# A ring of six joined rows instead of eight in the PEER layer, with the gate and gelu products made at the end of their own group

## What is computed

```python
def peer_block(xb, w_query, sub_keys, u_tab, v_tab):
    ...
    s1, i1 = lax.top_k(s[:, :, 0], PEER_TOPK)
    s2, i2 = lax.top_k(s[:, :, 1], PEER_TOPK)
    cand_s = (s1[..., :, None] + s2[..., None, :]).reshape(T, PEER_HEADS, PEER_TOPK * PEER_TOPK)
    ...
    top_s, pos = lax.top_k(cand_s, PEER_TOPK)
    e = jnp.take_along_axis(cand_i, pos, axis=-1)
    gate = jax.nn.softmax(top_s, axis=-1)
    act = jax.nn.gelu(jnp.einsum('thkd,td->thk', u_tab[e], xb).astype(jnp.float32))
    return jnp.einsum('thk,thkd->td', (gate * act).astype(xb.dtype), v_tab[e])
```

## Time and profile before

| | |
|---|---|
| time, median of 3 runs | 4445.95 us (4445.74 to 4453.35) |
| the profiled execution | 4451.51 us, of which the span of the profile is 4449.7 us |
| PE matmul busy | 3031.3 us (68%) |
| DVE busy | 2706.4 us (61%) |
| POOL busy | 1379.5 us (31%) |
| ACT busy | 1113.9 us (25%) |
| mean granted TensorE clock | 0.813 of full speed |
| moved by DMA | 1226.80 MB, of which 1132.54 MB by GpSimd's queue |

### The profile page before, as it was taken

The page is one execution under the profiler, slowest core; times in us unless marked ns, Lnnn a source line. Parts: engine busy times, 40 slices in busy tenths (PEclk is TensorE's granted clock), DMA queues, the critical chain, the costliest instruction groups (busy, mean ns, idle before and its releaser), DMA issues.

```text
span 4449.7 us, 52623 instructions
## 1 busy us (share of the span) xinstructions
PE 3031.3 (68%) x18622; PEld 1384.5 (31%) x18622; DVE 2706.4 (61%) x6853; ACT 1113.9 (25%) x2691; POOL 1379.5 (31%) x1229
## 2 busy tenths in 40 slices
PE   6999895377746766676676676676576666667656
PEld 3554342166624322222222222232132222222211
DVE  1710666633343767767767767776776776676775
ACT  1010342222112222322222322222232232222222
POOL 0000000000001544544444454453454444444421
PEclk8999787589868787787887788788778788778778
DMA  2111000000016999999999999999999999999974
GB/s 84 36 34 44 3 0 9 0 20 0 1 47 259 400 406 406 391 413 404 390 416 408 389 413 405 389 413 410 383 408 408 407 389 410 398 390 413 397 284 152
DMA packets 203348, 1226.80 MB, mean 276 GB/s; under 512 B 31424, under 2 KB 42336, under 8 KB 67584
## 3 DMA queue, kind: packets, MB, share of 16 engines
q0 software_dynamic: 160256, 1132.54, 62.9%
q1 hardware_dynamic: 42880, 91.61, 5.7%
HBM read 1211.00 MB, written 13.06 MB: 275 GB/s over the span
## 4 chain that ended last, share of the span: by engine, by line
DMA 30%; PE 14%; DVE 13%; issue 7%; POOL 5%; ACT 1%; SPq 0%; POOLq 0%; DVEq 0%; ACTq 0%
DMA uv_rows<-in_peer_uv,expert 29%; PE peer_y L1747 10%; POOL uv_rows L1294 4%; DVE uv_rows L1491 4%; PE peer_s L1632 2%; ACT diag L1613 1%; DVE same L1340 1%; DVE same L1338 1%; DVE pick L1342 1%; DVE p_x L1382 1%; PE peer_y L1741 1%; PE beside L1646 1%; PE peer_y L1721 0%; POOL pages_ring L1273 0%; DVE where L1318 0%
## 5 line engine op out<-in xcount | busy, mean ns | idle before, releaser
L1747 PE MATMUL peer_y<-uv_rows,diag 64*64 64x512 f32 x8192 | 1366.2, 801 | 973.6 <-ACT diag L1613 973.1
L1491 DVE CUSTOM_DVE_ANT_0 uv_rows<-uv_rows,p_h 128x1024 f32<-128x1024 f32 x1056 | 1293.0, 1225 | 760.5 <-DMA uv_rows<-in_peer_uv,expert 743.6
L1294 POOL DMA_INDIRECT uv_rows<-in_peer_uv,expert x1056 | 1215.3, 1151 | 1625.8 <-PE peer_y L1747 1083.5
L1747 PEld LDWEIGHTS peer_y<-uv_rows,diag 64*64 64x64 f32 x8192 | 333.0, 167 | 1773.6 <-ACT diag L1613 1247.6
L1613 ACT ACTIVATE diag<-p_ident,weights 128x128 f32<-128x128 f32 x1024 | 355.0, 394 | 1448.1 <-DVE weights L1366 1442.5
L328 PE MATMUL proj<-mix,w_in_tile 128*128 128x512 f32 x672 | 296.2, 599 | 19.4 <-issue 19.4
L1632 PE MATMUL peer_s<-wk,p_h2t 128*128 128x256 f32 x1152 | 280.7, 398 | 2.3 <-ACT p_h2t L1541 1.3
L1605 ACT ACTIVATE gelu<-hidden 128x2 f32<-128x2 f32 x528 | 107.4, 203 | 628.5 <-DVE hidden L1491 627.4
L1632 PEld LDWEIGHTS peer_s<-wk,p_h2t 128*128 128x128 f32 x1152 | 222.6, 199 | 113.3 <-issue 82.2
L774 POOL COPY v_c<-prc 128x192 f32 (+1 forms) x17 | 5.9, 345 | 740.8 <-POOLq L552 445.4
L1646 PE MATMUL beside<-w_out_rows,mix_block 128*128 128x512 f32 x288 | 153.2, 658 | 42.6 <-DMA p_ident<-in_ident 26.9
(11 more groups left out here) (321 smaller groups left out, 3837.5 us busy)
## 6 DMA issues: line engine op xcount, KB each, us to landing
w_out_rows<-in_w_out SPq DMA_DIRECT2D x72, 512.0 KB, 8.2
uv_rows<-in_peer_uv,expert POOLq DMA_INDIRECT x1056, 10.5
w_in_tile<-in_w_in SPq DMA_DIRECT2D x21, 512.0 KB, 3.6
uv_rows<-in_w_query SPq DMA_DIRECT2D x4, 2048.0 KB, 10.9
p_x<-in_x_rows SPq DMA_DIRECT2D x9, 512.0 KB, 11.4
mix<-in_xT SPq DMA_DIRECT2D x8, 528.0 KB, 6.7
mix_block<-scratch_mixed SPq DMA_DIRECT2D x8, 512.0 KB, 7.9
out_y<-p_x SPq DMA_DIRECT2D x8, 512.0 KB, 8.2
```

Of the source, the lines that this page charges most:

```text
L1294: pool.indirect_dma_start(out=uv[:, m % RING, :], out_offset=None, in_=io["peer_uv"], in_offset=bass.IndirectOffsetOnAxis(ap=expert[:, t % ...
L1491: nc.vector.tensor_tensor_reduce(out=uv[:, m % RING, 0:D], in0=uv[:, m % RING, 0:D], in1=h2[:, b % 2, :], scale=1.0, scalar=0.0, op0=ALU.m ...
L1747: ins = nc.tensor.matmul(Y[r][j][rows[c], :], diag[rows[r], (m + c) % (2 * GP), rows[r]], uv[rows[r], (m + c) % RING, D + j * 512:D + (j + ...
```

## The change

The ring has six slots (three groups), and `weigh(t, q)` stands at the end of its own group: behind both dots of it, behind `gates` and the group's piece of `choose`, and ahead of `add_values`, `normalise` and the work beside. The extra `weigh` behind the last turn goes. Nothing else is changed: the same instructions with the same shapes, the same number of picks.

```diff
-    RING = 8
+    RING = 6
...
                                                        accum_out=hid[:, g % 2, k:k + 1]).then_inc(dotted, 1)
-                        if k == 0 and g:
-                            weigh(*((t, q - 1) if q else (t - 1, groups_of(t - 1) - 1)))
                     if q == 0 and t + 1 < TURNS:
                         gates(t + 1)
                     if t + LEAD < TURNS:
                         for piece in range(4 * q // groups_of(t), 4 * (q + 1) // groups_of(t)):
                             choose(t + LEAD, piece)
+                    weigh(t, q)
                     if b and h == 0 and q == 0:
                         add_values(b - 1)
...
-            weigh(TURNS - 1, groups_of(TURNS - 1) - 1)
             add_values(NBLK - 1)
             normalise(NBLK - 1)
```

## The result

The changed kernel takes **4781.94 us** (median of 4 runs, 4770.57 to 4795.09) against 4445.84 us, a ratio of 1.0754 with a 95% interval of 1.0724 to 1.0785: 7.5% or some 336 us slower. The direction was forecast; the size (4635, at most 4755) was not. The profiled execution is the longest of the four, 4795.09 us with a span of 4793.3 us.

A forecast was written before the change was run, and what follows sets the result against it. The DMA transfers of the picks were taken as the bound. Eight blocks of 23.5 us, 188 us, on the profiled 4451.5 us give 4640; this execution being 5.6 us above the median, 4635 us, range 4490 to 4755.

The forecast's parts named there:

- DVE's stand for gelu: Even groups, 4 times a turn: DVE waits for gelu, hand-over some 0.35 us; 35 us of cover, so no cost.
- the block's start: PE starts 2.6 us sooner, add_values 1.15 us sooner, but the ring covers 5.2 us less: net 1.5 us more a block.
- the last block: Product ahead of one dot in six turns gains 7 us, later slots lose about as much: 0, within 8 either way.
- the refill's 9.54 us: First issue of a pair to its second pick's landing, read at a block's start; leaves 6.0 us for a hold after.
- The forecast's own holds: Second pick's landing to next issue into its slots: q = 5 9.45 us, q = 7 9.66, q = 1 7.8, q = 3 6.2.
- The clock: PE's mean clock 0.81, 1.2 GHz for two fifths of the time: 0.4 x 6.0 + 0.6 x 2.0 = 3.6 us a quiet turn.
- Turns with other traffic: Turn 3 of a block: a hold may last 10.2 us, nothing stalls; turns 1 and 4 cost 2 us each.
- The shorter refill: Refill in the running stretch is 7.5 us, so a hold may last 8.1 us: 4485 us; chance 0.14.
- the sum by the Trainium skill's fit: 2.0 us plus bytes over 436 GB/s: a pair lands in 6.8 us, holds may last 8.8 us, 28 us in all.
- The faster: Slots freed 1.15 us or more earlier, holds under the limit, DMA engines never starve in a turn: 4410 us; chance 0.06.
- the unchanged rival: Holds stay under the limit, but the block's start gives nothing as the ring is shorter: 4446 us; chance 0.04.
- The "much slower" rival: PE's granted clock falls from 0.79 to near 0.5, or DVE is late for landings: over 4760 us; chance 0.08.

The follow-up runs named there:

- The two filler runs: Changed kernel plus eight zero matmuls before the values of q = 5 and 7: in one PE quarter 4853.24 us; spread over four quarters 4761.01 us.
- The run on the pages: Changed kernel with the next block's K pages fetched in turn 5 instead of turn 3 of a block: 4770.12 us, ratio 1.0708.

## Why the prediction was wrong in size

**What held.** The DMA engines set the pace; six slots are too few for these holds; DVE's stand for gelu is free; the order alone is a gain (37 us were put on it at the block's start and in the last block, 49 measured for all of it). The share fell in quiet turns to 0.91 or 0.92, as written. The forecast put 2.0 to 6.0 us on a quiet turn, and all of this pointed at slower.

**Where the time came from.** As means over blocks 1 to 7, the eight turns of a block got longer by 4.2, 5.1, 7.7, 4.0, 3.5, 6.7, 6.1 and 7.3 us, 44.7 in all. Forecast were 5.1, 2, 3.6, 0, 2, 3.6, 3.6 and 3.6, which is 23.5. The spans add up: 7 x 44.7 (312.7 before rounding) for these blocks, 37.9 for the first, 3.0 for the last block, less 10.0 us by which this execution's first group landed earlier, is 343.6 us.

**The step that failed is the refill's 9.54 us**, taken as one number from a dry restart, with a stop charged only for each excess over a limit. The means over the 224 groups of the quiet turns, from each landing and issue in the traces:

| kernel or run | slots | hold (to the next issue), us | refill, us | a quiet turn, us |
|---|---|---|---|---|
| six slots, old order | 6 | 9.64 | 9.81 | 51.99 |
| the changed kernel | 6 | 7.60 | 10.64 | 48.73 |
| six slots, product first | 6 | 6.26 | 10.70 | 45.19 |
| the kernel before | 8 | 9.03 | 11.94 | 41.77 |
| eight slots, product first | 8 | 6.17 | 14.37 | 41.07 |

A turn is 8 x (hold + refill) / 3 with three pairs and / 4 with four: 48.6 us for the changed kernel, 48.73 measured. This is bookkeeping. Pairs take turns, so it comes out in every row, whatever the cause; it says only which term was mis-sized.

The forecast's own holds, with 8.3 for q = 2 and 5.4 for the three short ones (between 4.7 and 6.4 by its clock shares), are 57.6 us, 7.20 a group, 0.4 too small. With them and 9.54 the same formula gives 44.6 us, close to the forecast's 41.5 + 3.6 = 45.1. So the missing 1.1 us of refill is 8 x 1.1 / 3 = 2.9 us a turn, most of the 3.6 us by which a quiet turn came out longer than forecast, and the holds' 0.4 us is 1.1 us. The dry restart itself was sized well (8.92 us in the fence above), but nothing stood in front of it.

What it left out is **the pair in front**. In the changed kernel a refill took 9.2 us where the pair before it had less than 2 us left to land when it was issued (27 groups), 10.4 us where that had 4 to 5 us left (41), and 11.6 us where it had 6 to 7 (46). On the mean 1.75 of the three pairs are on their way (3 x 10.64 / 18.24), so the mean refill lies above the dry restart's. The table shows the same with six slots: from the old order to the new the hold fell by 2.04 us and the refill grew by 0.83. The shorter the holds, the more the pairs meet on their way, and with eight slots and a DMA share of 1.00 the refill takes up all that the ring leaves.

The bunching adds little to the mean. Pairs issued less than 5 us behind the last took 11.65 us (76 groups), but those more than 8 us behind took 9.40 (40), and those 5 to 6.5 us behind, around the mean distance of 6.1, took 10.52 (52), against 10.64 for all. With the product first the distances are more even (59 groups under 5 us, only 5 over 8), and the refill is still 10.70; in the old order they are less even, and it is 9.81.

**The clock.** I mixed slow and fast holds by the mean clock, two fifths to three fifths. The groups with the longest holds run at 1.2 GHz nearly always: over the quiet turns the granted clock for the values of q = 5 is 0.52 after the change and was 0.52 before it, which could have been read from the trace before. The mix took 0.6 x 1.74 us off q = 5, 7 and 1, and a third of that sum is 1.0 us a turn, the smaller error. The two filler runs show that work of PE ahead of these values raises it (0.67 and 0.88); how much time a full clock there would give back is not shown.

**Turns with other traffic** were to be covered (turn 3: nothing). They got 3.5 to 5.1 us longer. In turn 3 the refill averages 12.97 us from issue: other transfers share the way with the picks, so they lengthen the round too and don't only fill its pauses. The reasoning that allowed a hold of 10.2 us there kept 9.54 for the refill. The run on the pages leaves open how much of this could be covered elsewhere; they are a third of the other traffic in that turn (1.6 of 4.8 MB).

**The block's start** was forecast at 1.5 us more, with add_values 1.15 us sooner; in block 3 it starts 2.0 us after PE is done, as it now waits for a landing. Turn 0 still lengthened by 4.2 us only, near the 5.1 forecast for it.

**The last block** stayed within its bounds: its last values end 180.1 us after the eighth block's last landing instead of 177.1, and the DMA engines idle as before (DMA share 0.46).

**The rivals.** The shorter refill (4485) is refuted, and with it the sum by the Trainium skill's fit, DMA: Bandwidth & Descriptors, section on the anatomy of a DMA on the GpSimd path: a pair in 6.8 us is what no refill here came near, the shortest of blocks 1 to 7 is 8.1 us. That page's fit is of one transfer, and this case has a queue of them. The faster and the unchanged rival fell with it. The "much slower" rival had the size (over 4760) but not the cause: the mean clock of block 3 fell by 0.01 only, and DVE was not late.

## What to carry to other kernels

With a ring of buffers in front of a saturated DMA, count the round: hold plus refill, averaged over the buffers that take turns, against the ring's depth times the transfer's own period; as soon as the round is longer, every microsecond of any hold costs its share, and a saturated profile gives no warning of how near the limit is. A refill read at a dry restart (9.54 us) is too short for the mean, since in a running stretch the pair in front is still on its way (9.8 to 10.7 us with six slots). One read in a saturated stretch (11.94 us before) is no limit either, since there it grows to fill the ring. A limit that lies between the two is a range, and a hold inside it should be priced as a cost. Shorten the hold before spending memory: putting the product right behind its dots made seven slots do 1.0% better than eight had done before.

## What was not expected of the hardware

The granted TensorE clock has a place in the program: in the same turn it was 0.52 for the values of q = 5 and 1.00 for those of q = 2, which stand right behind the scores, before the change and after (means over the quiet turns). A mean clock of 0.8 says nothing about a single step of the path. And matmuls on 64 rows by 64 columns that all sit in one quarter of the array took 6.65 us for 15 records, while 16 of the same shape spread over its quarters take 1.95 to 3.69 us.
